# A product moved from GpSimd to VectorE, evictions moved to ScalarE, and matmul groups placed apart in a stick-breaking attention stage

## The reference, cut to what matters

```python
for i in range(S // Q_BLOCK):                      # 8 blocks of 128 queries
    z = einsum('bhqd,bhkd->bhqk', qb, kb) * inv_sqrt       # only keys up to the block's end
    mask = s_idx < t_idx
    log1m = where(mask, -softplus(z), 0.0)
    after = cumsum(log1m, axis=3, reverse=True) - log1m
    logw = log_sigmoid(z) + after
    w = where(mask, exp(where(mask, logw, 0.0)), 0.0)
    outs.append(einsum('bhqk,bhkd->bhqd', w, vb))
```

## Time and profile before

| | |
|---|---|
| time, median of 3 runs | 2699.89 us (2698.12 to 2707.13) |
| the profiled execution's own time | 2698.92 us |
| its span, first to last instruction | 2696.8 us |
| busy: PE, PEld, DVE, ACT, POOL | 94%, 76%, 42%, 31%, 23% of the span |
| chain that ended last | PE 75%, DVE 13%, issue 4%, ACT 3%, POOL 2% |
| mean granted TensorE clock | 0.971 of full speed |

### The profile page before, as it was taken

How to read it: one execution, slowest core, us unless ns; L and a number is a source line. 1 busy time by engine, 2 the same in 40 slices (tenths; PEclk the granted TensorE clock), 3 DMA queues, 4 the chain that set the end, 5 groups by cost and what they waited for, 6 DMA issues and landing times.

```text
span 2696.8 us, 31180 instructions
## 1 busy us (share of the span) xinstructions
PE 2524.3 (94%) x12551; PEld 2038.3 (76%) x12551; DVE 1137.5 (42%) x2129; ACT 824.4 (31%) x1484; POOL 608.8 (23%) x305
## 2 busy tenths in 40 slices
PE   7999989879999999999999978888899999999998
PEld 6667877668877887887887756656778888888886
DVE  2698997743524224224237046663541111111115
ACT  3556647641321111111123224442431021111112
POOL 2012210001122222222223234454212122222220
PEclk9999989889999999999999999998999999999999
DMA  5016441232123223224412200001321111111122
GB/s 155 16 52 191 157 141 55 98 117 68 31 71 121 75 71 125 71 71 125 126 63 79 78 16 17 16 17 63 103 79 61 39 55 48 39 55 47 57 76 101
DMA packets 195719, 205.45 MB, mean 76 GB/s; under 512 B 13788, under 2 KB 143340, under 8 KB 195576
## 3 DMA queue, kind: packets, MB, share of 16 engines
q1 hardware_dynamic: 195576, 203.46, 23.9%
HBM read 170.88 MB, written 32.56 MB: 75 GB/s over the span
## 4 chain that ended last, share of the span: by engine, by line
PE 75%; DVE 13%; issue 4%; ACT 3%; POOL 2%; DMA 1%; SPq 1%; POOLq 0%; DVEq 0%; ACTq 0%
PE bank L444 15%; PE bank L446 14%; PE bank L445 14%; PE bank L469 8%; PE bank L471 8%; PE bank L470 8%; PE bank L1306 2%; DVE junk L1021 1%; DVE res L1241 1%; DVE rest L2132 1%; POOL wl L425 1%; DVE score L994 1%; PE bank L1216 1%; PE bank L488 1%; PE bank L1280 1%
## 5 line engine op out<-in xcount | busy, mean ns | idle before, releaser
L425 POOL TENSOR_TENSOR wl<-raw,wh 128x1024 fp32r<-128x1024 f32 x189 | 455.9, 2430 | 1915.5 <-ACT wh L416 1915.5
L444 PE MATMUL bank<-yh,wh 128*128 128x512 f32 x1536 | 602.8, 392 | 12.1 <-DVE ql L2027 6.2
L446 PE MATMUL bank<-yh,wl 128*128 128x512 f32 x1536 | 599.0, 390 | 0.0
L445 PE MATMUL bank<-yl,wh 128*128 128x512 f32 x1536 | 598.9, 390 | 0.0
L416 ACT ACTIVATE wh<-raw 128x1024 fp32r<-128x1024 f32 x189 | 196.1, 1054 | 545.4 <-PE bank L471 242.5
L444 PEld LDWEIGHTS bank<-yh,wh 128*128 128x128 f32 x1536 | 289.3, 188 | 80.4 <-issue 8.3
L446 PEld LDWEIGHTS bank<-yh,wl 128*128 128x128 f32 x1536 | 289.1, 188 | 60.5
L445 PEld LDWEIGHTS bank<-yl,wh 128*128 128x128 f32 x1536 | 289.4, 188 | 59.5 <-issue 0.2
L1733 DVE TENSOR_TENSOR sil_gate<-sil_gate,bank 128x512 f32<-128x512 f32 x44 | 30.3, 688 | 359.2 <-PE bank L446 358.9
L1733 DVE TENSOR_TENSOR sil_gu<-sil_gu,bank 128x512 f32<-128x512 f32 x44 | 30.3, 688 | 326.0 <-PE bank L446 213.4
L1753 DVE TENSOR_TENSOR res<-bank,res 128x512 f32<-128x512 f32 x112 | 76.0, 689 | 214.2 <-PE bank L471 214.2
(11 more groups left out here) (289 smaller groups left out, 4179.7 us busy)
## 6 DMA issues: line engine op xcount, KB each, us to landing
raw<-in_w_cond SPq DMA_DIRECT2D x48, 512.0 KB, 3.8
raw<-in_w_gu SPq DMA_DIRECT2D x44, 512.0 KB, 5.2
raw<-in_w_down SPq DMA_DIRECT2D x44, 512.0 KB, 3.6
raw<-in_w_in SPq DMA_DIRECT2D x40, 512.0 KB, 4.0
raw<-in_w_gate SPq DMA_DIRECT2D x22, 512.0 KB, 3.9
raw<-in_w_up SPq DMA_DIRECT2D x22, 512.0 KB, 3.9
res<-in_x SPq DMA_DIRECT2D x16, 512.0 KB, 9.0
raw<-in_w_out SPq DMA_DIRECT2D x16, 512.0 KB, 3.6
```

The source lines that it names most:

```text
L425: pool.i.tensor_tensor(wl[n % NU][:, :], raw[u % NRAW][:, :], wh[n % NU][:, :].bitcast(F32), ALU.subtract).then_inc(*po.up(("wl", u)))
L444: pe.i.matmul(bank[:, :], a, a_h[:, s], start=k == 0, stop=False)
L445: pe.i.matmul(bank[:, :], a, a_l[:, s], start=False, stop=False)
L446: last = pe.i.matmul(bank[:, :], b, a_h[:, s], start=False, stop=k == 7)
```

## The change

Four edits, all in that stage:

1. The share is computed by VectorE right behind its own scan, no longer by GpSimd. GpSimd is left with the low parts of weight tiles and the seven splits.
2. All turned pieces are evicted by ScalarE; VectorE evicts none.
3. TensorE weighs a pair in odd steps, t - 7 and t - 6 in step t: half a pair later, behind both turns.
4. The projections stand elsewhere. Group 0 begins with two of its four, the others follow after u = 1 and u = 5. Of a later group's four, q half 1, k half 1 and k half 0 stand after u = 16, 18 and 22 of the group before, and q half 0 after u = 4 of the group itself (for group 3 after u = 23 of group 2). Weight tiles come k first, then q.

```diff
-            plan += [("F", "w_in_2", 128 * h), ("F", "w_in_2", 512 + 128 * h)]
+            plan += [("F", "w_in_2", 512 + 128 * h), ("F", "w_in_2", 128 * h)]
...
-        BESIDE = {16: (0, 1), 19: (1, 1), 22: (0, 0), 23: (1, 0)}
+        BESIDE = {16: (0, 1), 18: (1, 1), 22: (1, 0)}
+        FIRST = {1: (1, 0), 5: (0, 0)}
...
                 if h == 0:
-                    for half in (1, 0):
-                        for n in range(2):
-                            yield "qk", 0, n, half
+                    for n in range(2):
+                        yield "qk", 0, n, 1
                 for u in range(PER_PAIR):
                     yield "piece", PER_PAIR * h + u, None, None
+                    if h == 0 and u in FIRST:
+                        yield "qk", 0, *FIRST[u]
                     if h < 3 and u in BESIDE:
                         yield "qk", h + 1, *BESIDE[u]
+                    if 0 < h < 3 and u == 4 or h == 2 and u == 23:
+                        yield "qk", h + (u == 23), 0, 0
...
-            if 0 <= t - LATE - 1 < N_PIECE and (t - LATE) % 2 == 0:
-                pe_stick_weigh(t - LATE - 2)
+            if 0 <= t - LATE - 3 < N_PIECE and t % 2:
+                pe_stick_weigh(t - LATE - 3)
...
-            pe.wait_ge(*po.after(("share", t)))
+            pe.wait_ge(*dv.after(("share", t)))
...
-            pe.wait_ge(*av.after(("stickt", t)))
-            pe.wait_ge(*dv.after(("stickt", t + 1)))
+            pe.wait_ge(*av.after(("stickt", t + 1)))
...
-            if 0 <= u < N_PIECE and u % 2 == 0:
+            if 0 <= u < N_PIECE:
                 n = pieces[u][4]
                 act.wait_ge(*mm.after(("stickt", u)))
...
-                dve.i.tensor_copy(wts[u % 4][:, 0:n], uses.held["stickt", u][:, 0:n]).then_inc(*dv.frees(uses, ("stickt", u)))
+                s_ = took[t % 5]
+                dve.wait_ge(*av.after(("z", t)))
+                dve.wait_ge(*dv.after(("product", t)))
+                dve.i.tensor_tensor(s_[:, 0:n], s_[:, 0:n], r[:, 1:n + 1], ALU.mult).then_inc(*dv.up(("share", t)))
...
-                pool.i.tensor_tensor(s_[:, 0:n], s_[:, 0:n], rest_of[t % 4][:, 1:n + 1], ALU.mult).then_inc(*po.up(("share", t)))
...
-                for n in range(2):
+                for n in (1, 0):
                     sp_feed(qk2_units[h][n])
```

More of the change, by code:

```diff
@@ L2050, in pe_stick_logits @@
             pe.wait_ge(*dv.after(("qk2", h, 1, c0 // 512)))
-            pe.wait_ge(*dv.after(("qk2", h, 1, i // 4)))
+            pe.wait_ge(*dv.after(("qk2", h, 0, i // 4)))
             (qh, ql), (kh, kl) = qs, ks
@@ L2104, in act_stick @@
                 if t >= 4:
-                    act.wait_ge(*po.after(("share", t - 4)))
+                    act.wait_ge(*dv.after(("share", t - 4)))
                     act.wait_ge(*dv.after(("product", t - 2)))
@@ L2178, in act_split @@
             act.wait_ge(*dv.after(("sticko", k, 0) if k < 4 else ("map", k - 4, 1)))
-            act.wait_ge(*mm.after(("qk2", 3, 1, 0)))
+            act.wait_ge(*mm.after(("qk2", 3, 0, 0)))
             act.i.activation(yh[:, 1024 * k:1024 * k + 1024], src, ACT.Copy).then_inc(*av.up(("split", k)))
@@ L2215, in pool_sticks @@
                 else:
-                    pool_stick(t)
                     if t in split_at:
```

## The result

The changed kernel takes 2663.37 us (median of 4 runs, 2660.83 to 2665.65), the one before 2700.46 us beside it. The ratio is 0.9858, with a 95% interval of 0.9838 to 0.9879: 33 to 44 us gained. The profiled execution took 2664.65 us, its span is 2662.5.

The account below looks back on a forecast made before the run. Late hand-over bounds it: TensorE idles 32.8 us before the weighing, behind VectorE's scans. Gains of 31.3 up to group 3 and 1.0 there, less 3 for low clock, make 29.3 off 2698.92: 2670 us, range 2654 to 2692.

Parts of the forecast that it names:

- The two phases of a group: Groups with projections: VectorE bounds up to the next group's first projection, TensorE from there; 58.3 us a group against 67.
- the sum: Whole stage: 31.3 us gained up to group 3, 1.0 in group 3, less 3 for low clock: 29.3.
- The price of a piece: On VectorE, column copy, scan and share of a 512 piece cost 2.04 us, bounds 1.35 to 2.8.
- the share's 0.70: On VectorE, a share instruction of 512 columns takes about 0.70 us, of which 0.08 lies under the next.
- the low clock: TensorE falling to 1.2 GHz after idling: 1 us added a group in groups 0 to 2, 3 in all.
- A split's price: Group 3: each GpSimd split takes 1.8 us from VectorE, 12.6 for seven.
- its forecast gain of 1.0: Group 3, no projections and VectorE the longest queue: 58.4 us against 59.4 before.
- I cost the later weighing and ScalarE's 48 added evictions at nothing: Covered by VectorE's 4.1 us a pair; if uncovered, under 0.5 us each, some 2 us a group.
- Rival D: ScalarE's single queue of sigmoids, evictions and read-outs gives each group's gain back: 2698 us, chance 0.05.
- Rival A: TensorE bounds all along, no bubble, no low clock: 2656 us, chance 0.13.
- Rival C: TensorE falls to 1.2 GHz and stays there in VectorE-bound stretches: 2703 us, or 2730 if further; chance 0.08.
- Rival B: A piece on VectorE costs more than 2.04 us; at 2.3 for 512, 16 us more: 2686 us, chance 0.14.

Follow-up runs that it names:

- e8: Changed kernel with weight tiles of groups 0 to 2 behind k half 0 and q half 0 made later, at the projection after u = 18: 2654.53 us, ratio 0.9812.
- e7: Changed kernel with GpSimd's seven splits computing only 8 of their 1024 columns (wrong low parts): 2652.82 us, ratio to the kernel before 0.9820.
- e12: Changed kernel with late weight tiles, group 3's splits on VectorE and the share back on GpSimd: 2643.44 us, ratio to the kernel before 0.9787.
- e4: Changed kernel with edit 2 alone undone, odd turned pieces evicted by VectorE again: 2713.54 us, ratio to the kernel before 1.0049.
- e11: Kernel before with edit 2 alone, all turned pieces evicted by ScalarE: 2675.68 us, ratio to the kernel before 0.9909.
- e5: Changed kernel with edit 3 alone undone, pairs weighed early, in even steps between the turns: 2675.24 us, ratio to the kernel before 0.9893.
- e3: Changed kernel with edit 1 alone undone, the share back on GpSimd: 2662.76 us, ratio to the kernel before 0.9858.
- e2: Kernel before with edit 4 alone, the new places of projections and weight tiles: 2704.69 us, ratio to the kernel before 1.0019.
- e1: Changed kernel with edit 4 undone, projections and weight tiles in their old places: 2676.05 us, ratio to the kernel before 0.9910.

## Why the prediction was right, and where it was not

- **The two phases of a group** were right. VectorE bounds from the first logits to the first projection, TensorE from there; 58.3 was forecast for a group, 57.2 measured, and e8 and e7 each gave back about what the sum says of VectorE's path. Without its splits group 3 takes 45.8 us (e7), which is the sum's own 58.4 less 12.6.
- **The price of a piece** was right (2.04, measured 2.05), and so was the share's 0.70.
- **The sum** was 29.3 and the stage gave 32.1. The term mis-sized is the low clock, 3 us for groups 0 to 2. The granted clock was 1.00 in groups 1 and 2, where TensorE never waited longer than 1.0 us, and 0.97 in group 0, where one projection took 6.1 instead of 5.7. The rest of the sum agrees by luck in part. The prediction counts from the end of one group's last projection to the next; those ends are at 1637.38, 1694.58 and 1758.93, the first two 1.3 us before the first logits. So counted, group 0 took 74.9 (73.5 forecast), group 1 57.2 (58.3), group 2 64.4 (65.4) and group 3 59.8 (58.4): errors of 1.0 to 1.4 us that cancel to 0.6.
- **A split's price** was 1.8 and is 2.0: seven scans or shares in group 3 took 3.31, 2.47, 2.84, 2.60, 3.28, 3.38 and 2.34 us, which is 14.1 more than the same shapes alone. Group 3 so took 59.9 instead of 58.4: its forecast gain of 1.0 was a loss of 0.5. By the rule of the Trainium skill ("SBUF — State Buffer", section "Who interferes with whom"), that either instruction excludes the other for its whole length, seven tiles of 2.37 us would have cost 16.6; the measured 14.1 lies between that and the 12.6 of the sum. Where scan and product follow each other the rule is also a little too strict: the two alone last 1.27 + 1.09 = 2.36, and a piece took 1.97 (e12).
- **A row was misread** for group 3. GpSimd's 26.5 us of 29 were called the longest queue, but VectorE has 28.0 in the same row. Over the whole group before the change GpSimd was the busier one, 53.0 against 49.0:

```profile
1792.50:1851.90 59.40, 41.68 (x335) 27.76 (x334) 49.04 (x66) 34.49 (x73) 52.95 (x32) 0.86 0.04 10
```

- **"I cost the later weighing and ScalarE's 48 added evictions at nothing"** left no gap in the sum, though no run prices it: TensorE waits 17.8 us for these evictions in the changed kernel, in group 1 only in the stretch that VectorE bounds. But the step saw in them only a cost and took the wait for VectorE as one of the weighing alone. The evictions hold the two turned banks as well, and they carry the most (e4, e11). Without edit 2 the change is a loss of 0.5% (e4), without edit 3 a gain of 1.1% (e5), without edit 1 the same 1.4% (e3).
- **Rival D** (ScalarE's queue gives it back) fell: its 33.3 us of work in group 1's 57.2 leave room. **Rival A** was not reached: TensorE has 52.2 us of work in group 1's 57.2; e8 brings it to 51.9 in 53.5. **Rival C** did not come: its low level showed almost only in group 3 (a mean clock of 0.77), and there e7 leaves nothing for it to have cost. **Rival B** fell with the piece's 2.05.
- The whole time moved by 37 us and the forecast was 30; about 5 of the difference lie outside the stage, where nothing was forecast. They are not explained; the stage's start alone moves by 7 us between executions.

## What to carry to other kernels

When an engine waits for an eviction, ask what stands ahead of that eviction in its engine's queue and which bank it holds; moving half of the evictions out from behind the scans (e11, 20.1 us of the stage) was worth more than moving a product between engines (e3, nothing). Spread other work into a waiting stretch only after the hand-over is mended: the same places cost 5 us before (e2) and were worth 10 after (e1). Price a GpSimd tile beside VectorE instructions with two SBUF operands by what it takes from them, some 2 us of 2.4 here, and put it where VectorE is not the bound.

## What the runs showed of the hardware that I had not expected

A scan of VectorE and a product of GpSimd that meet slow each other down, but not by their whole lengths: a piece takes some 0.4 us less than the two alone, at each of the three widths seen. In e12 a piece with a scan of 512 (1.27 us alone) takes 1.97 us beside products of 512 (1.09 alone), 1.52 beside 256 (0.63 alone) and 1.29 beside 128 (0.41 alone). One long tile costs the instruction beside it 1.9 to 2.2 us of its 2.4 (a scan of 512 takes 3.3 instead of 1.27). Seven tiles blocked 14.1 us and freed 14.1 when cut short (e7). And TensorE's mean granted clock in group 3 rose from 0.77 to 0.96 with the same matmuls in e7, where it waited 8.8 us in the group instead of 14.3.
